# Hymba streaming step on one core: the gathered token rows of an expert block land on other partitions

## The reference, cut to what matters

```python
def expert_block(args):
    xb, e = args
    return (jax.nn.silu(xb @ lp['w1'][e]) * (xb @ lp['w3'][e])) @ lp['w2'][e]
```

## Time and profile before

| | |
|---|---|
| time, median of 3 runs | 1324.8 us (1324.03 to 1327.75) |
| span of the profiled execution, first to last instruction | 1322.7 us, that is 2.1 us under the median |
| PE busy | 1226.0 us, 93% |
| DVE, ACT, POOL busy | 419.6, 334.8, 279.3 us |
| moved by DMA | 278.64 MB, 17.84 MB of it by the indirect transfers |
| mean granted PE clock | 0.980 |

### The profile page before, as it was taken

How to read it: one execution, slowest core, us unless ns; L and a number is a source line. 1 busy time by engine, 2 the same in 40 slices (tenths; PEclk the granted TensorE clock), 3 DMA queues, 4 the chain that set the end, 5 groups by cost and what they waited for, 6 DMA issues and landing times. The chain is left out here.

```text
span 1322.7 us, 31681 instructions
## 1 busy us (share of the span) xinstructions
PE 1226.0 (93%) x13264; PEld 868.3 (66%) x13264; DVE 419.6 (32%) x907; ACT 334.8 (25%) x781; POOL 279.3 (21%) x401
## 2 busy tenths in 40 slices
PE   8999999998899999999999879997799899888886
PEld 4554444445565666666666679663699898888883
DVE  2433311025654555554643651111011111111111
ACT  3522110124444545545444100110000000000001
POOL 2220000103312312212111012222122332232321
PEclk9999999999998999999999889998899999999999
DMA  9611211142202202201032979999999999999996
GB/s 344 252 56 40 65 65 41 47 158 68 81 17 66 81 17 66 81 17 59 17 120 105 411 277 368 372 364 373 363 390 369 371 376 376 391 377 378 379 397 232
DMA packets 45276, 278.64 MB, mean 211 GB/s; under 512 B 10280, under 2 KB 15400, under 8 KB 32252
## 3 DMA queue, kind: packets, MB, share of 16 engines
q1 hardware_dynamic: 37088, 254.80, 50.0%
q0 software_dynamic: 6800, 17.84, 5.8%
q10 hardware_dynamic: 1296, 4.72, 1.0%
HBM read 250.49 MB, written 29.83 MB: 212 GB/s over the span
## 5 line engine op out<-in xcount | busy, mean ns | idle before, releaser
L1119 PE MATMUL psum<-arena 128*128 128x512 f32 (+1 forms) x576 | 241.4, 577 | 3.3 <-DVE arena L1878 2.4
L1187 PE MATMUL psum<-arena 128*64 128x80 f32 (+1 forms) x5632 | 224.6, 241 | 14.3 <-DMA arena<-in_w 10.6
L1187 PEld LDWEIGHTS psum<-arena 128*64 128x64 f32 x5632 | 216.6, 139 | 22.6 <-issue 10.9
L1119 PEld LDWEIGHTS psum<-arena 128*128 128x128 f32 x576 | 108.9, 191 | 127.3 <-issue 123.5
L1252 PE MATMUL psum<-arena 128*64 128x96 f32 (+1 forms) x2816 | 115.2, 242 | 23.9 <-issue 15.7
L1252 PEld LDWEIGHTS psum<-arena 128*64 128x64 f32 x2816 | 111.5, 137 | 26.8 <-issue 17.7
L1020 PE MATMUL psum<-arena 128*128 128x512 f32 x288 | 126.9, 593 | 1.8 <-DVE arena L2111 1.0
L1777 POOL DMA_INDIRECT out_y<-arena,index_now x54 | 75.3, 1394 | 178.8 <-ACT arena L1598 112.2
L1658 POOL TENSOR_SCALAR small<-small 128x2 f32<-128x2 f32 (+4 forms) x44 | 10.3, 234 | 448.9 <-DVE small L1859 164.8
L1020 PEld LDWEIGHTS psum<-arena 128*128 128x128 f32 x288 | 53.3, 190 | 63.2 <-issue 61.6
L1598 ACT ACTIVATE arena<-psum,slot_gate 96x1024 f32<-96x1024 f32 x22 | 24.4, 1111 | 277.2 <-PE psum L1262 277.2
(11 more groups left out here) (255 smaller groups left out, 1344.6 us busy)
## 6 DMA issues: line engine op xcount, KB each, us to landing
arena<-in_w SPq DMA_DIRECT2D x94, 2048.0 KB, 29.6
z_rows<-arena SPq DMA_DIRECT2D x27, 256.0 KB, 2.0
arena<-z_rows SPq DMA_DIRECT2D x9, 768.0 KB, 5.2
arena<-in_w_in SPq DMA_DIRECT2D x3, 2048.0 KB, 22.6
arena<-in_xT_rows SPq DMA_DIRECT2D x9, 512.0 KB, 10.6
arena<-in_x_rows ACTq DMA_DIRECT2D x9, 512.0 KB, 6.2
arena<-in_x_rows SPq DMA_DIRECT2D x9, 512.0 KB, 6.3
out_y<-arena SPq DMA_DIRECT2D x9, 512.0 KB, 2.6
```

The lines of the kernel that those rows point to most:

```text
L1119: ins = pe.matmul(o[:, 0:w], xT[n][:, k, :], w_in[:, at_ + k * w:at_ + (k + 1) * w], start=(k == 0), stop=(k == KD - 1))
L1187: ins = pe.matmul(o[c:c + CT, j * EB:j * EB + rows], w[:, k, j * P + c:j * P + c + CT], x[:, k, 0:rows], start=(k == 0), stop=(k == KD - 1))
```

## The change

It changes where the gathered rows land, and what reads them. `TURN` is 32.

- The first 64 rows of a block go to partitions 32 to 95 instead of 0 to 63. The rows above 64 go to partitions 0 upward instead of 64 upward. The three first blocks and the spare ones are gathered as before.
- PE always transposes 96 partitions, where it transposed 64, 80 or 96. The partitions that hold no row of this block hold rows of an earlier one; their columns are not read.
- DVE takes the columns 32 to 95 into columns 0 to 63 of `xeT`, and, for a block over 64, the columns 0 upward into columns 64 upward by a second instruction. From there on everything is as before.

```diff
-            def gather_transposes(s, b, arrived, count, rows):
+            def gather_transposes(s, b, arrived, count):
...
-                    ins = pe.transpose(bank(0, 2)[:, k * P:k * P + rows], xe[s][0:rows, k * P:(k + 1) * P],
-                                       ident[0:rows, 0:rows])
+                    ins = pe.transpose(bank(0, 2)[:, k * P:k * P + EB], xe[s][0:EB, k * P:(k + 1) * P], ident[0:EB, 0:EB])
...
-                fetch(xe[s][0:rows if parts == 1 else ET], now_tok[s][0:rows if parts == 1 else ET], signal)
+                if parts == 1 and rows > ET:
+                    fetch(xe[s][0:rows], now_tok[s][0:rows], signal)
+                else:
+                    fetch(xe[s][TURN:EB], now_tok[s][0:ET], signal)
                 if parts == 2:
-                    fetch(xe[s][ET:rows], hi_tok[s][0:rows - ET], signal)
+                    fetch(xe[s][0:rows - ET], hi_tok[s][0:rows - ET], signal)
...
-            def xeT_take(s, b, rows):
+            def xeT_take(s, b, rows, turned=True):
                 dve.wait_ge(xeT_full, b + 1)
-                TT(xeT[s][:, :, 0:rows], bank(0, 2).rearrange("p (k t) -> p k t", t=P)[:, :, 0:rows], bc(g_ffn, [P, KD, rows]),
-                   ALU.mult).then_inc(xeT_read, 1)
+                o = bank(0, 2).rearrange("p (k t) -> p k t", t=P)
+                if not turned:
+                    TT(xeT[s][:, :, 0:rows], o[:, :, 0:rows], bc(g_ffn, [P, KD, rows]), ALU.mult).then_inc(xeT_read, 1)
+                    return
+                ins = TT(xeT[s][:, :, 0:ET], o[:, :, TURN:EB], bc(g_ffn, [P, KD, ET]), ALU.mult)
+                if rows > ET:
+                    ins = TT(xeT[s][:, :, ET:rows], o[:, :, 0:rows - ET], bc(g_ffn, [P, KD, rows - ET]), ALU.mult)
+                ins.then_inc(xeT_read, 1)
```

More of the change, by code:

```diff
@@ L73 @@
 ROUND = 12582912.0
+TURN = EB - ET
 PART = KD * FF
@@ L1279, in expert @@
                     hidden_back(q)
-                    gather_transposes(1 - s, b + 1, xe_in[1 - s], gathers_of(p + 1) + rows_more, CAPS[p + 1]) if p < NE - 1 else None
+                    gather_transposes(1 - s, b + 1, xe_in[1 - s], gathers_of(p + 1) + rows_more) if p < NE - 1 else None
                     downs_read(b - 2, p - 2)
@@ L1286, in expert @@
                     down(SETS[q], b - 1, w2_in[SETS[q]], loads_of(q) + more, CAPS[q])
-                    gather_transposes(1 - s, b + 1, xe_in[1 - s], gathers_of(p + 1) + rows_more, CAPS[p + 1])
+                    gather_transposes(1 - s, b + 1, xe_in[1 - s], gathers_of(p + 1) + rows_more)
                 hidden_3(SETS[p], s, b, w3_in[SETS[p]], loads_of(p) + more, rows)
@@ L1290, in expert @@
                     turn_back(b - 1, tiled(q))
-            gather_transposes(0, 0, xe_in[0], 16, EB)
+            gather_transposes(0, 0, xe_in[0], 16)
             hidden_1(0, 0, 0, w1_in[0], 16, EB)
-            gather_transposes(1, 1, xe_in[1], 16, EB)
+            gather_transposes(1, 1, xe_in[1], 16)
             hidden_3(0, 0, 0, w3_in[0], 16, EB)
@@ L1319, in _ @@
                     with pe.If(j < total):
-                        gather_transposes(0, NE + j, ov_xe, 16 * j + 16, EB)
+                        gather_transposes(0, NE + j, ov_xe, 16 * j + 16)
                         hidden_1(0, 0, NE + j, ov_w, 48 * j + 48, EB)
@@ L2396, in turn @@
                 if p < NE - 1:
-                    xeT_take(1 - p % 2, b + 1, CAPS[p + 1])
+                    xeT_take(1 - p % 2, b + 1, CAPS[p + 1], p + 1 >= FIRST)
                 if by_tokens(p):
@@ L2401, in turn @@
                     hidden(b)
-            xeT_take(0, 0, EB)
+            xeT_take(0, 0, EB, False)
             list_order()
             silu(0, EB)
-            xeT_take(1, 1, EB)
+            xeT_take(1, 1, EB, False)
             hidden(0)
@@ L2427, in _ @@
                     with dve.If(j < total):
-                        xeT_take(0, NE + j, EB)
+                        xeT_take(0, NE + j, EB, False)
                         silu(NE + j, EB)
```

## The result

The changed kernel takes 1289.99 us (median of 4 runs, 1287.87 to 1294.22) against 1324.41 us before, a ratio of 0.974 (95% interval 0.972 to 0.976). It is 34.4 us faster.

The account below looks back on a forecast made before the run. It took the DMA queue's drain rate as the bound between 884 and 961 us and behind 1051 us. Savings of 10 + 2.5 + 13.3 = 25.8 us, cut to 23, gave 1324.8 - 23 = 1302 us, range 1293 to 1325.

Parts of the forecast that it names:

- The gather windows: Sign in 80-row blocks: rate while a gather is in flight, 390 GB/s or more if fully cured, 332 if not.
- two blocks: Sign late in the expert loop: the chain's two-block period falls from 35.8 us to about 33.5.
- PE's idle time behind 1051 us: Sign at the end of the expert loop: PE's waiting falls from 26.8 us to about 13.
- the worth of one gather: In the expert loop, a 4.8 us gather stretch at 332 instead of 432 GB/s loses 1.11 us, bounds 1.0 and 1.4.
- How much of 1.11 us a gather reaches the end of the kernel depends on the stretch.: Expert loop: savings counted as 10 us up to 961 us, 2.5 in the 96-row blocks, 13.3 behind 1051 us.
- the 96-row stretch: Expert-loop stretch of 96-row blocks where PE waits 4.3 us; about 4.4 us offered, 2.5 us counted.
- the remaining four gathers: Gathers said to fall in the stretch that PE sets; nothing counted for them in the sum of 25.8 us.
- a tenth taken off for the rows above 64: Gathers: about a tenth of rows still arrive bunched on 16 neighbouring partitions, so 25.8 us becomes 23 us.
- The cover that the prediction names: PE's idle time hides wider transposes, without it up to 4.4 us; the split take on DVE without cover 3 us.
- Writes into the low partitions: Gathers, unlike scatters, write low SBUF partitions beside the weights; claimed reason for 332 GB/s against about 369.
- This spreads them: Gathered rows on 32 to 95, half in each SBUF half, relieve colliding DMA engines; full cure 23 us, 48%.
- the half cure: Rival: gathers rise only to about the scatter's rate, 0.5 to 0.6 us each, 1312 to 1314 us; 26%.

Follow-up runs that it names:

- base 36: The changed kernel with the first 64 gathered rows on partitions 36 to 99 instead of 32 to 95, the rest from 0 upward: 1315.43 us.
- the step from 36: The changed kernel with 16-row gathers from block 3 on, the first DMA's rows on every fourth partition 36 to 96, the second's one higher: 1287.2 us.
- bases 36 and 16: The changed kernel with the first 64 rows on partitions 36 to 99 or 16 to 79 instead of 32 to 95: 1315.43 and 1318.93 us.
- bases 0 and 64: The changed kernel with the first 64 rows on partitions 0 to 63 or 64 to 127 instead of 32 to 95: 1325.27 and 1325.91 us.
- The steps of 16 rows: The changed kernel with 16-row gathers from block 3 on, on every fourth partition from 32, 0 or 36: 1276.15, 1283.01 and 1287.2 us.

## Why the prediction was wrong in size

**Right: what bounds the kernel.** The queue drains at the rate that was lost in the gathers, and a faster gather brings the end forward. The gather windows rose from 334 to 431 GB/s, the landing fell from 9.5 to 8.2 us (8.5 was forecast), two blocks take 31.65 us (about 33.5), and PE's idle time behind 1051 us fell to 4 us (about 13).

**Right: the worth of one gather.** The prediction took 1.11 us. The nine gathers of blocks 11 to 19 gave 1.14 us each (in a trace that has the stops of PE told above, which may hold it down), all 29 gave 34.4/29 = 1.19 us. Worked out anew from the windows of 5.4 us it is 5.4 x (1 - 334/431) = 1.2 us.

**Wrong: "How much of 1.11 us a gather reaches the end of the kernel depends on the stretch."** This is the step that failed. The prediction gave 9 gathers to the time before 961 us, let the 96-row stretch keep 2.5 of 4.4 us, because PE "can give up at most 4.3 us" there, and let "the remaining four gathers" fall where PE sets the time, at nothing. The trace of before has 12 gathers up to 961 us, 5 up to 1051 and 12 behind. The last before either bound and the first behind it:

```profile
942.74 0.99 POOL L1760 DMA_INDIRECT arena<-xn_rows,index_now  x1 [0.81 <-POOL index_now L1768]
...
969.16 1.00 POOL L1760 DMA_INDIRECT arena<-xn_rows,index_now  x1 [0.80 <-POOL index_now L1768]
...
1044.59 1.02 POOL L1760 DMA_INDIRECT arena<-xn_rows,index_now  x1 [0.84 <-POOL index_now L1768]
...
1064.32 1.02 POOL L1760 DMA_INDIRECT arena<-xn_rows,index_now  x1 [0.85 <-POOL index_now L1768]
```

At 1.15 us that would be 13.8, 5.8 and 13.8 us; the stretches gave 13.9 (2.4 + 4.8 + 6.7, the 2.4 of doubtful origin), 5.0 and 15.6. Where PE was the busy one the saving was not lost: the queue went on moving more there (399 instead of 377 GB/s), so the loads got ahead of PE by what was saved, and PE cashed it at its next wait. The nine gathers in the middle, for which the prediction counts 3.6 us, gave 10.2. Without the discount, 29 x 1.11 = 32.2 us and 1292.6 us, within 3 us of the result. Of the 11.4 us that the forecast of 23 us fell short, 32.2 - 25.8 = 6.4 are this discount, 2.8 the tenth below, and 2.2 the worth of a gather.

**Wrong: a tenth taken off for the rows above 64.** 25.8 became 23 us. The spread of those rows changed nothing, and the windows of after, which hold both parts of a gather, are at the rate of weights alone. For real rows in all the places there would be something to it; most of these indices are empty.

**Right while the queue is the bound: the transposes and the take cost nothing.** 1325.27 with both and the old place. By the groups of after, eight transposes take 28.3/32 = 0.88 us (0.93 forecast), the two takes 0.681 + 0.414 = 1.10 us (1.1 forecast). The cover that the prediction names has become thin, though: PE is busy for 215.03 of 219 us, and the chain runs over the transposes; what they cost there no run shows.

```profile
L1179 PE MATMUL psum<-ident,arena 96*128 96x96 f32 x256 | 28.3, 255 | 6.1 <-DMA arena<-xn_rows,slot_out 6.1
...
L2358 DVE TENSOR_TENSOR arena<-psum,small 128x512 f32<-128x512 f32 x29 | 19.7, 681 | 0.0
L2360 DVE TENSOR_TENSOR arena<-psum,small 128x256 f32<-128x256 f32 x18 | 7.4, 414 | 0.0
```

**Half right: the cause.** That the place of the rows makes a gather slow was right. "Writes into the low partitions" was wrong: partitions 64 to 127 are as slow. "This spreads them" was not enough either: base 36 and the step from 36 are nearly as widely spread as the fast places. That the base chosen was 32 and not another with rows in both halves was luck, as far as the reason given for it goes: 36 would have brought 10 us.

What fits the fast places is that a DMA engine's rows are cheap where they land in the groups of four partitions into which this engine writes its weights. With 64 rows in 16 shares of four, base 32 does that for all shares, bases 36 and 16 for none, bases 0 and 64 for half of them while the other half pile on the same engines' groups: 1290 against 1315, 1319, 1325 and 1326 us.

The Trainium skill, page "DMA: Bandwidth & Descriptors", section "The descriptor swizzle", gives for a transfer over 128 partitions the engine as 8 x (partition >> 6) + ((partition >> 2) & 7), engine 0 writing partitions 0 to 3 and 32 to 35. The runs agree in that the two places at which all rows are an engine's own by it are the two fastest, 1290 and 1276 us; no view names the engine that wrote a row, so the assignment itself is inferred. The page "SBUF — State Buffer", section "Door 1: The DMA port swizzle", by which the half cure was sized, counts the ports that a transfer reaches. By its map the base 36 reaches 15 of 16 and should be nearly as good as 32. The runs say 10 us against 34, and the measurement decides: reaching the ports is not enough.

Neither count orders the slower places by itself. The bases of 64 rows fall in the order of the ports reached by that map (16, 15, 12, 8 and 8: 1290, 1315, 1319, 1325 and 1326 us), not in that of the own shares, since 0 and 64 with half of them own are the slowest. The steps of 16 rows fall in the order of the own rows (16, 8, 0: 1276, 1283, 1287 us), not in that of the ports (16, 8, 15). So both seem to count; what is shown is only that all rows at the supposed own place is best, at the same bytes and nearly the same spread.

Open are five things: how the two counts go together, how 32 rows are dealt, what an empty index costs the queue, what stops PE in the middle of a product in four of the kernels, and the mechanism inside the chip by which a row in a neighbour's group slows the weights of all.

## What to carry to other kernels

When the DMA queue is never dry, a saving in it is worth its full size wherever in the program it falls, also where another engine is the busy one, as long as that engine still has waits behind it in which to cash the saving (here 48.6 us of them before): multiply by all the events, compare the sum with the waits that are left, and don't discount by stretch. Look at the rate within single events of a stream, not at its busy share, which was 1.01 to 1.03 at 334 as at 431 GB/s, and 1.00 in a kernel that PE bound. When small rows are mixed into a stream that fills all the partitions, try the place at which each engine would write rows where it writes the stream (here 64 rows on 32 to 95 by one DMA), and measure the neighbouring places, since four partitions off lost three quarters of it. Before the time of a control is used, look at what its trace waits for: three of them here were bound by PE at their end, and their times say nothing of the queue.

## What the runs showed of the hardware

- The place of gathered rows in SBUF changes what the weight stream beside them loses: 64 rows of 4 KB at base 32 nothing that the windows show (434 and 428 GB/s in all), at base 0 between a sixth and a quarter (338 and 330 before, 356 and 315 with the place put back), at base 36 a fifth (346 and 349).
- One indirect DMA of 64 rows and two of 32 to the same 64 partitions are not the same: 1290 against 1321 and 1325 us. An extra empty DMA does not lower the rate (402 GB/s from 884 to 961 us), two of 32 real rows do (375).
- An index out of bounds moves nothing, but reads: 896 of them added 3.67 MB to the bytes read from HBM, a row of 4 KB each.
- The busy share of the DMA engines was 1.00 to 1.03 whether they moved 334 or 431 GB/s, and also where PE never waited for them.
- In four kernels PE stops for 0.3 to 0.4 us in the middle of a product, without a releaser: 22 times from 1051 to 1250 us without rows, 43 times in the control with an extra empty DMA a block.
- With 16 rows a DMA the place alone moved the kernel by 21.5 us at the same bytes (1297.62 and 1276.15).
